# Linear-attention buffers moved out of the conv history's bytes, conv halves written later, and the sample rows' conv as products and one sum

## The reference

```python
za, zq, zk, zv, zg, zr = split_cols(z, [2 * D_CONV, GLA_DK, GLA_DK, GLA_DV, GLA_DV, GLA_RANK])
ya, conv_new = conv_module(za, conv_prev, conv_w, conv_b, conv_ln_g, conv_ln_b)
yb, gla_new = gla_mixer(zq, zk, zv, zg, zr, gla_prev, gla_w_gate, gla_b_gate, gla_g_norm)
return jnp.concatenate([ya, yb], axis=-1), conv_new, gla_new
```

## Time and profile before

| | |
|---|---|
| time, median of 3 runs | 2952.89 us (2947.61 to 2955.87) |
| time of the profiled execution | 2945.37 us |
| its span in the profile | 2943.7 us |
| PE busy | 2768.6 us (94%) |
| DVE busy | 1397.8 us (47%) |
| ACT busy | 1162.7 us (39%) |
| granted clock of PE, mean | 0.949 |

### The profile page before, as it was taken

The page is one execution under the profiler, slowest core; times in us unless marked ns, Lnnn a source line. Parts: engine busy times, 40 slices in busy tenths (PEclk is TensorE's granted clock), DMA queues, the critical chain, the costliest instruction groups (busy, mean ns, idle before and its releaser), DMA issues.

```text
span 2943.7 us, 48112 instructions
## 1 busy us (share of the span) xinstructions
PE 2768.6 (94%) x20153; PEld 2534.3 (86%) x20153; DVE 1397.8 (47%) x2026; ACT 1162.7 (39%) x1488; POOL 86.1 (3%) x116
## 2 busy tenths in 40 slices
PE   5899967989999999999999899889899999999998
PEld 1788955878888888898999899579899999999998
DVE  1699736344444433444444445534545544444444
ACT  2333254234343322334433445433544433444433
POOL 1000000010000000000000000001000000000000
PEclk7999986899999999999999999589999999999999
DMA  9677782675777688777644444114344434444343
GB/s 400 269 274 277 277 140 100 247 271 219 280 286 284 257 322 319 284 281 283 229 147 157 164 165 150 35 55 172 118 167 171 152 139 178 168 162 171 138 164 130
DMA packets 75771, 603.50 MB, mean 205 GB/s; under 512 B 21029, under 2 KB 22373, under 8 KB 24050
## 3 DMA queue, kind: packets, MB, share of 16 engines
q1 hardware_dynamic: 75634, 601.54, 55.8%
HBM read 592.01 MB, written 9.49 MB: 204 GB/s over the span
## 4 chain that ended last, share of the span: by engine, by line
PE 85%; DVE 5%; DMA 4%; ACT 3%; issue 2%; SPq 1%; POOL 1%; DVEq 0%; POOLq 0%; ACTq 0%
PE ps L599 25%; PE ps L601 24%; PE ps L600 24%; PE ps L625 5%; DMA pre_ring<-in_w_ada 2%; DMA aring<-in_w_ada 2%; DVE w_lo L1321 1%; DVE cacc L1410 1%; PE ps L610 1%; PE ps L841 1%; SPq L456 1%; ACT tn L1135 1%; ACT w_hi L979 1%; PE ps L638 0%; POOL ssq L553 0%
## 5 line engine op out<-in xcount | busy, mean ns | idle before, releaser
L1321 DVE TENSOR_TENSOR w_lo<-raw,w_hi 128x2048 fp32r<-128x2048 f32 (+1 forms) x402 | 835.6, 2080 | 1156.3 <-ACT w_hi L979 1156.3
L599 PE MATMUL ps<-act_hi,w_hi 128*128 128x288 f32 x4352 | 1303.3, 299 | 46.0 <-DVE act_lo L1508 30.9
L600 PE MATMUL ps<-act_hi,w_lo 128*128 128x288 f32 x4352 | 1288.7, 296 | 0.0
L601 PE MATMUL ps<-act_lo,w_hi 128*128 128x288 f32 x4352 | 1283.9, 295 | 0.0
L979 ACT ACTIVATE w_hi<-raw 128x2048 fp32r<-128x2048 f32 (+1 forms) x402 | 699.5, 1741 | 1110.2 <-PE ps L601 1104.2
L599 PEld LDWEIGHTS ps<-act_hi,w_hi 128*128 128x128 f32 x4352 | 820.2, 188 | 107.0 <-issue 91.7
L601 PEld LDWEIGHTS ps<-act_lo,w_hi 128*128 128x128 f32 x4352 | 823.9, 189 | 0.0
L600 PEld LDWEIGHTS ps<-act_hi,w_lo 128*128 128x128 f32 x4352 | 821.9, 189 | 0.0
L599 PE MATMUL ps<-hid_hi,w_hi 128*128 128x288 f32 x1408 | 420.5, 299 | 8.6 <-DVE w_lo L1321 8.6
L600 PE MATMUL ps<-hid_hi,w_lo 128*128 128x288 f32 x1408 | 416.7, 296 | 0.0
L601 PE MATMUL ps<-hid_lo,w_hi 128*128 128x288 f32 x1408 | 415.3, 295 | 0.0
(11 more groups left out here) (264 smaller groups left out, 1401.4 us busy)
## 6 DMA issues: line engine op xcount, KB each, us to landing
aring<-in_w_ada SPq DMA_DIRECT2D x176, 1024.0 KB, 7.9
raw<-in_w_gu SPq DMA_DIRECT2D x88, 2048.0 KB, 8.2
raw<-in_w_dn SPq DMA_DIRECT2D x64, 1408.0 KB, 5.9
raw<-in_w_ab SPq DMA_DIRECT2D x20, 2048.0 KB, 8.0
raw<-in_w_out SPq DMA_DIRECT2D x16, 2048.0 KB, 8.3
raw<-in_w_cd SPq DMA_DIRECT2D x13, 2048.0 KB, 8.2
pre_ring<-in_w_ada SPq DMA_DIRECT2D x16, 1024.0 KB, 9.4
aring<-in_state_glaT SPq DMA_DIRECT2D x4, 1024.0 KB, 9.2
```

The source lines that it names most:

```text
L599: pe.matmul(bank, w_hi[:, h, cols], hi[:, kt, :], start=begin, stop=False)
L600: pe.matmul(bank, w_lo[:, h, cols], hi[:, kt, :], start=False, stop=False)
L601: mm = pe.matmul(bank, w_hi[:, h, cols], lo[:, kt, :], start=False, stop=end)
L1321: dve.tensor_tensor(w_lo[:, h, 0:w], raw[:, par, h * w:(h + 1) * w], w_hi[:, h, 0:w].bitcast(F32), ALU.subtract).then_inc(split_done, 1)
```

## The change

Four things are changed.

1. The GLA buffers lie in `w_hi[:, 1]` and `w_lo[:, 1]`, the second places of the split weights, which hold nothing between the last z step and the output projection. The waits for the conv's copies and stores ahead of the heads go. The split of the output projection's first second half moves from head 0 to behind head 3, behind waits for all stores.
2. The conv's result goes to `act_hi` and `act_lo` in head 0, behind the gate of head 1 (`conv_high`, `conv_low`), where that split was. SP issues the conv stores behind the state loads of heads 0 and 1.
3. In the conv, a tile's sample columns are made by 4 products of 8 x 31 (one for each new token) into `taps_prod`, one sum over the taps and one addition of the bias, in place of 31 instructions. The prompt columns keep 31, each of which now adds to the result of the one just ahead of it.
4. Squares, `stat`, `rstd` and the affine of the layer norm move ahead by about a step; squares have four slots; the affine of the sample columns goes to DVE (`samples_affine`); loops over 8 sequences become one instruction.

```diff
--- before.py
+++ after.py
...
             free_lo = sb("free_lo", [P, KT * T], stack=a)
...
         raw = sb("raw", [P, 2, SLOT])
-        w_hi = sb("w_hi", [P, 2, SLOT // 2], F32R)
-        w_lo = sb("w_lo", [P, 2, SLOT // 2], F32R)
+        with ExitStack() as a:
+            w_hi = sb("w_hi", [P, 2, SLOT // 2], F32R, stack=a)
+        with ExitStack() as a:
+            sb("under_w_hi1", [P, SLOT // 2], stack=a)
+            gs = sb("gs", [P, 4, 256], stack=a)
+            vtok = sb("vtok", [P, 2, 256], stack=a)
+            os_tok = sb("os_tok", [P, 2, 256], stack=a)
+        sb("w_hi_home", [P, SLOT])
+        with ExitStack() as a:
+            w_lo = sb("w_lo", [P, 2, SLOT // 2], F32R, stack=a)
+        with ExitStack() as a:
+            sb("under_w_lo1", [P, SLOT // 2], stack=a)
+            vtok_s = sb("vtok_s", [P, 256], stack=a)
+            kltok = sb("kltok", [P, 2, P], stack=a)
+            klm = sb("klm", [P, 2, P], stack=a)
+            att = sb("att", [P, 2, P], stack=a)
+            att_s = sb("att_s", [32, 32], stack=a)
+            rowmask = sb("rowmask", [P, 2], stack=a)
+        sb("w_lo_home", [P, SLOT])
         aring = sb("aring", [P, 2, 4 * ADA_N])
...
-        with ExitStack() as a:
-            sb("under_z", [P, 24 * T], stack=a)
-            gs = sb("gs", [P, 4, 256], stack=a)
-            vtok = sb("vtok", [P, 2, 256], stack=a)
-            os_tok = sb("os_tok", [P, 2, 256], stack=a)
...
+        def square_of(q):
+
+            if isinstance(q, int) and SQUARES[1] <= q < SQUARES[2]:
+                return (sqb[:, 0], sqb[:, 1], sg[:, 0], sg[:, 1])[q % 4]
+            return sqb[:, q % 2]
...
-                sp.wait_ge(conv_ready, CT)
-                sp.dma_start(o["conv_p"], uext[:, :, NP_TOK:UW]).then_inc(conv_stored, 16)
-                for j in range(CT):
-                    sp.dma_start(o["conv_s"][:, j], rows_s(j)[:, :, TS:SW]).then_inc(conv_stored, 16)
                 for h in range(HEADS):
...
+                    if h == 1:
+                        store_conv()
                     if h >= 1:
                         store_states(h - 1)
                 store_states(HEADS - 1)
                 sp.wait_ge(state_stored, 16 * HEADS)
+
+            def store_conv():
+
+                sp.wait_ge(conv_ready, CT)
+                sp.dma_start(o["conv_p"], uext[:, :, NP_TOK:UW]).then_inc(conv_stored, 16)
+                for j in range(CT):
+                    sp.dma_start(o["conv_s"][:, j], rows_s(j)[:, :, TS:SW]).then_inc(conv_stored, 16)
...
-                    if seg.kind == "z" and ls == 2:
-                        stat()
...
+                    if seg.kind == "z" and ls == 1:
+                        stat()
...
-            def conv_squares():
-                for j in range(CT):
+            def conv_squares(js):
+                for j in js:
                     q = 16 + j
-                    wait_square(q)
-                    act.activation(sqb[:, q % 2, 0:NP_TOK], y_all[:, j], ACT.Square)
-                    act.activation(seqs(sqb[:, q % 2, NP_TOK:T]), y_all_s[:, j], ACT.Square).then_inc(sq_ready, 1)
+                    act.wait_ge(sq_added, q - 3)
+                    act.activation(square_of(q)[:, 0:NP_TOK], y_all[:, j], ACT.Square)
+                    act.activation(seqs(square_of(q)[:, NP_TOK:T]), y_all_s[:, j], ACT.Square).then_inc(sq_ready, 1)
...
-                    for y in (y_all[:, j], y_all_s[:, j]):
-                        ins = act.activation(y, y, ACT.Identity, scale=vec[:, gj:gj + 1], bias=vec[:, bj:bj + 1])
+                    y = y_all[:, j]
+                    ins = act.activation(y, y, ACT.Identity, scale=vec[:, gj:gj + 1], bias=vec[:, bj:bj + 1])
                 ins.then_inc(conv_affined, 1)
...
+                    if seg.kind == "z" and ls == 1:
+                        act.wait_ge(centred, 1)
+                        conv_squares(range(4))
+                    if seg.kind == "z" and ls == 2:
+                        act.wait_ge(normed, 1)
+                        conv_affine()
                     if nxt:
                         split(nxt, n + 1, 1 - par, 0)
+                    if seg.kind == "z" and ls == 1:
+                        conv_squares(range(4, CT))
...
-                        stat_rstd(CT * P)
-                        act.wait_ge(normed, 1)
-                        conv_affine()
+                        act.wait_ge(conv_affined, 2)
+                        for k in range(2):
+                            conv_silu(k)
...
-                        act.wait_ge(centred, 1)
-                        conv_squares()
...
+                        stat_rstd(CT * P)
...
                 gate_terms(0)
-
-                act.wait_ge(conv_y, CT // 2)
-                act.activation(act_hi[:, 0:CT, 0:NP_TOK], y_all, ACT.Copy)
-                for s in range(NSEQ):
-                    ins = act.activation(act_hi[:, 0:CT, NP_TOK + TS * s:NP_TOK + TS * (s + 1)], y_all_s[:, :, s], ACT.Copy)
-                ins.then_inc(mixhi_done, CT)
                 gate_exps(0)
 
-                act.wait_ge(act_ready, KT + CT)
-                act.wait_ge(conv_stored, 16 * (CT + 1))
...
-                        split(after, after.n0, after.n0 % 2, 1)
+                        conv_high()
...
+                act.wait_ge(gstate_stored, 16 * HEADS)
+                act.wait_ge(conv_stored, 16 * (CT + 1))
+                split(after, after.n0, after.n0 % 2, 1)
...
+                acc = cacc[:, 0:NP_TOK]
+                acc_s = cacc[:, NP_TOK:T].rearrange("p (t b) -> p t b", b=NSEQ)
                 if 0 in taps:
                     if not (isinstance(j, int) and j == 0):
                         dve.wait_ge(conv_ready, j)
                     if L.n:
                         L.wait(L.n)
+                    ws = vec[:, bass.ds(j * TAPS + w, TAPS)].unsqueeze(1).to_broadcast([P, NSEQ, TAPS])
+                    for at_t in range(TS):
+                        ins = dve.tensor_tensor(taps_prod[:, at_t], rows_s(j)[:, :, at_t:at_t + TAPS], ws, ALU.mult)
+                    marks[1] = L.mark(ins)
                 for k in taps:
                     wk = flat_at(vec, j * TAPS + (w + k))
-                    for s in range(2):
-                        row = taps_s(j, k) if s else at(uext, j, k, k + NP_TOK)
-                        acc = seqs(cacc[:, NP_TOK:T]) if s else cacc[:, 0:NP_TOK]
-                        out = acc if k < TAPS - 1 else taps_s(j, 0) if s else at(uext, j, 0, NP_TOK)
-                        if marks[s]:
-                            L.wait(marks[s])
-                        if k == 0:
-                            ins = dve.tensor_scalar(out, row, wk, flat_at(vec, j + VEC["conv_b"]), ALU.mult, ALU.add)
-                        else:
-                            ins = dve.scalar_tensor_tensor(out, row, wk, acc, ALU.mult, ALU.add)
-                        if k == TAPS - 1 and s:
-                            ins.then_inc(conv_ready, 1)
-                        else:
-                            marks[s] = L.mark(ins)
+                    row = at(uext, j, k, k + NP_TOK)
+                    if k == 6:
+                        L.wait(marks[1])
+                        marks[1] = L.mark(dve.tensor_reduce(acc_s, taps_prod[:], AX.X, ALU.add))
+                    if k == 16:
+                        L.wait(marks[1])
+                        dve.tensor_scalar(taps_s(j, 0).rearrange("p b t -> p t b"), acc_s, flat_at(vec, j + VEC["conv_b"]),
+                                          None, ALU.add)
+                    if k == 0:
+                        marks[0] = L.mark(dve.tensor_scalar(acc, row, wk, flat_at(vec, j + VEC["conv_b"]), ALU.mult, ALU.add))
+                        continue
+                    L.wait(marks[0])
+                    if k < TAPS - 1:
+                        marks[0] = L.mark(dve.scalar_tensor_tensor(acc, row, wk, acc, ALU.mult, ALU.add))
+                    else:
+                        dve.scalar_tensor_tensor(at(uext, j, 0, NP_TOK), row, wk, acc, ALU.mult, ALU.add).then_inc(conv_ready, 1)
...
-                    if seg.kind == "z" and ls == 2:
-                        for k in range(2):
...
+                    if seg.kind == "z" and ls == 1:
+                        dve.wait_ge(rstd_ready, 2)
+                        apply_stat(y_all, y_all_s, rstd, ALU.mult).then_inc(normed, 1)
+                        samples_affine()
...
-                for s in range(NSEQ):
-                    cols = by[:, NP_TOK + TS * s:NP_TOK + TS * (s + 1)].unsqueeze(1).to_broadcast([P, CT, TS])
...
+                return dve.tensor_tensor(y_s, y_s, seqs(by[:, NP_TOK:T]).unsqueeze(1).to_broadcast([P, CT, NSEQ, TS]), op)
...
+                gj, bj = VEC["conv_ln_g"], VEC["conv_ln_b"]
+                rows = y_all_s
+                dve.wait_ge(normed, 1)
+                g, b = (vec[:, k:k + CT].unsqueeze(2).unsqueeze(3).to_broadcast([P, CT, NSEQ, TS]) for k in (gj, bj))
+                L.link(dve.tensor_tensor(rows, rows, g, ALU.mult))
```

(13 more changed lines are left out.)

39 lines of the change are left out of this document (15 added, 24 removed).

## The result

The changed kernel takes 2924.14 us, the median of 4 runs (2921.99 to 2930.57), against 2951.52 for the kernel before on the same chip (2947.61 to 2955.87). The ratio is 0.991, 95% interval 0.9888 to 0.9932: faster by 0.9%. The profiled execution took 2922.46 us where that of before took 2945.37, 22.9 less; the forecast for it was 2920.7, and for the median 2928.2, 4 above what was measured.

What follows compares the result with a forecast made beforehand. PE was taken as the bound, busy nearly throughout, so other engines' edits pay only where PE waits. Terms -9.1 - 18.2 + 0.7 + 0 + 0.5 + 1.4 = -24.7 turn the median 2952.9 into 2928.2 us; range 2920 to 2940.

Steps and rivals of the forecast that it cites:

- Layer norm earlier: First mixer's z steps: PE no longer waits 5.2 us for POOL's sum, `adarow` and the drain come earlier; -9.1 us.
- signs listed: Trace observations named beforehand as showing the prediction right or wrong, such as PE waiting over 8 us for `w_lo`.
- The wait for the stores: Ahead of head 0: `vtok` follows the gate's exponentials directly instead of waiting for the conv stores; -18.2 us.
- SP's order: State loads go ahead of the conv stores; head 1's `gs` write meets the stores' end; +0.5 us, bounds 0 to +10.
- The rival of 2938: Stores come back as a wait inside the heads: head 1's `gs` waits 10 us; 2938 us, chance 0.12.
- Head 0: Conv copies replace a split of the same 2048 columns, plus one 256-column instruction each on ACT and DVE; +0.7 us.
- The split at the end: Split moved behind head 3 is ready before PE needs it, with 6 us of cover; nothing added.
- The conv on DVE: First 16 taps take 10.3 to 10.4 us against 9.0, delaying PE in the opening; +1.4 us.
- DVE becomes the bound in the gate steps: Rival: sums and products at the scan's rate cost 2.7 us more a tile; +9.8 us, 2938 us, chance 0.07.
- links are free: Rival: chained conv taps on DVE cost nothing extra, only instruction count matters; -26.4 us, 2926.5 us, chance 0.08.
- last rival: The wait ahead of the heads was not for the stores, so they start as late; 2944 us, chance 0.01.

Runs made afterwards that it cites:

- buffers only: Kernel before with the new GLA buffers, new SP order, conv parts behind head 1's gate and moved split, old layer norm and conv: 2933.52 us, ratio 0.9949.
- old conv: Changed kernel with the taps of prefix and samples in turns, as in the kernel before: 2922.78 us, ratio 0.9913.
- stores first: Changed kernel, its buffers kept, with SP's nine conv stores ahead of the two state loads again: 2945.51 us, ratio 0.9991.
- late products: Changed kernel with the samples' products between taps 24 and 27 and their sum ahead of tap 28: 2923.02 us, ratio 0.9899.
- parts ahead: Conv's high and low parts ahead of head 0 again: changed kernel 2923.54 us, ratio 0.9914; with late products and prefix taps in two sums, 2917.87 us, 0.9896.
- old norm's place: Changed kernel with two square buffers, `stat` a step later, sample affine on ACT and normalization in step 2: 2934.2 us, ratio 0.9959.
- second profile: Changed kernel, nothing altered, run and profiled once more on another chip: 2928.0 us, ratio 0.9913 of the kernel before.

## Why the prediction was right

**Layer norm earlier, -9.1.** Right. A to B shows 9.19 between the changed kernel and the one with the old place, and 9.05 between buffers only (295.97) and old conv (286.92), which differ in this alone there. The affine took 4.04 where I had put 4, and `adarow` began at 404.35, where the sum's 401.4, the 2.2 of the conv and a start 0.7 later give 404.3. Of the signs listed, `adarow` was to come 7 to 8 us earlier than before and came 6.1 earlier, and head 0's keys near 418 came at 419.63: both misses are the conv's term and that start.

**The wait for the stores, -18.2.** Right: B to C fell by 18.36. That it was the stores' the view of ACT didn't say (its 18.18 us stand as "issue"); DVE's waits in the kernel before, from 443 us on, do, for its own first write into those bytes:

```profile
DVE att L1605 <- DMA out_conv_s<-uext: 14.8, 1, 14.8
```

What I had not weighed is how much of it SP's new order carries. I priced that order as a small cost, +0.5, and gave no rival in which it was left as it was; the kernel with the stores first shows 19.00 us on it.

**SP's order, +0.5 with 0 to +10 as bounds.** It cost nothing. The stores' end was put at 444 and the last thing in that queue, `gs`, landed at 444.4; but head 1 wrote `gs` at 448.09 and not at 444.9, as head 0 began and ran later than in the sum. So the two did not meet, by 3.7 us. The rival of 2938, with chance 0.12, had the stores end 10 us later; by these rows that would have cost 6 and not 10. It was nearer than the result tells: in the other eight traces with this order `gs` is written 0.8 us (late products) to 9.3 us (buffers only) after its store has landed, always behind a wait for PE.

**Head 0, +0.7.** Right for the work, though the head grew by 1.35 (21.43 to 22.78). The rest is the granted clock, which the sum had no term for. The eight products of values and keys at the start of the head show it, in the kernel before and in the changed one:

```profile
447.74 1.13 PE L776 MATMUL ps<-vtok,kltok 64*128 64x256 f32 x8
```

```profile
423.38 1.71 PE L800 MATMUL ps<-vtok,kltok 64*128 64x256 f32 x8
```

In the rows of stretches the granted clock was 1.00 there in the kernel before, and 0.65 in the changed one:

```profile
447.70:448.90 1.20, 1.20 (x13) 0.79 (x9) 0.00 (x0) 1.01 (x2) 0.00 (x0) 1.00 0.00 0
```

```profile
423.40:425.10 1.70, 1.70 (x10) 1.20 (x9) 0.00 (x0) 1.53 (x3) 0.00 (x0) 0.65 1.78 34
```

These eight are in the chain: DVE's copy to `gs` waits for them. They take 1.14 to 2.08 us in the seven traces with the same head, and C to D less their time is 20.98 to 21.07 in all seven, which explains the spread of the table. In the kernel before it is 21.43 - 1.13 = 20.30, so the conv parts cost 0.77. With the parts ahead it is 20.13 and 20.49; the 0.36 between these two lies in PE's outputs behind the eight, from its first product of `att` to its first of `klm`: 6.82 us (431.24 to 438.06) and 7.18 (423.65 to 430.83), the first 0.8 us at a granted clock of 1.00 and of 0.81.

**The split at the end, nothing.** Right: the low half was done at 510.60, PE wanted it behind the pair of 514.55.

**The conv on DVE, +1.4.** This is the term that was mis-sized: it is +2.2 (289.12 - 286.92), and +2.3 by the other pair (298.31 - 295.97). Each instruction was priced rightly. What failed is the step "so the front-loaded 1.4 delays PE there": it counted the first tile's 16 taps and stopped. With it went a slip in the sum, "in all of a tile it is 17.6 against 17.3": 10.4 for the first 16 taps, 15 x 0.51 for the rest and the bias make about 18.1. DVE's timeline has 10.42 + 2.11 + 5.60 = 18.13 for the first tile, against 17.30 before, so a tile costs 0.8 more and not 0.3. PE's stops in the opening before were 2.69 and 1.50, beside a common one of 1.39; now they are 4.20, 1.16 and 1.07, as PE's timeline of the changed kernel has them:

```profile
134.99 0.58 PE L623 MATMUL ps<-act_hi,w_hi 128*128 128x288 f32 x1 [4.20 <-DVE w_lo L1348]
...
156.86 0.40 PE L623 MATMUL ps<-act_hi,w_hi 128*128 128x288 f32 x1 [1.16 <-DVE w_lo L1348]
...
164.59 0.37 PE L623 MATMUL ps<-act_hi,w_hi 128*128 128x288 f32 x1 [1.07 <-DVE w_lo L1348]
```

The first grew by 1.5. The second tile has its products in front as well, ahead of a low half that PE also waits for, and that was left out. DVE's timeline shows it; first the changed kernel, then the same `w_lo` before:

```profile
148.27 1.39 DVE L1430 TENSOR_TENSOR taps_prod<-uext,vec 128x248 f32<-128x248 f32 x4
...
162.16 2.29 DVE L1348 TENSOR_TENSOR w_lo<-raw,w_hi 128x2048 fp32r<-128x2048 f32 x1
```

```profile
159.22 2.28 DVE L1321 TENSOR_TENSOR w_lo<-raw,w_hi 128x2048 fp32r<-128x2048 f32 x1
```

From the start of the first tile's conv to there are 162.16 - 122.14 = 40.02 us against 159.22 - 121.42 = 37.80, so 2.2 more. Piece by piece: +1.50 for the first 16 taps, -0.67 for the rest of the first tile, +1.80 for the second tile's first piece with its products and sum, -0.43 for its next taps. Over the first two tiles DVE is the bound, so the whole sum of its work between two low halves counts, not only what is front-loaded; the late products tell the same in another way. PE's stops are no measure of the delay by themselves: with the same conv, old norm's place and stores first have three stops that sum to 6.7 us, without the one of 1.16, since PE ran at a granted clock of 0.78 and 0.75 from 138 to 146 us.

That the loss ended there was luck. DVE's period of two gate steps, 28.9 us before, is now 186.32 - 156.72 = 29.6, against PE's 29.7:

```profile
156.72 0.45 DVE L1383 SCALAR_TENSOR_TENSOR sg<-ps,sg 128x288 f32<-128x288 f32 x1
...
186.32 0.45 DVE L1383 SCALAR_TENSOR_TENSOR sg<-ps,sg 128x288 f32<-128x288 f32 x1
```

The prediction wrote that 0.3 more fits; 0.7 did, with 0.1 to spare. The rival in which DVE becomes the bound in the gate steps, at chance 0.07, needed no price like the scan's, only a little more than what was measured.

The rival in which the links are free is refuted by the 0.513 against 0.395 of the two chains. The Trainium skill, "VectorE: DVE Perf Modes", section "The DRAIN you can't avoid", has a semaphore between chained operations cost nothing extra; the measurement, 0.12 us a link, decides against it.

**The sum.** -9.1 + 2.2 - 18.4 + 1.4 = -23.9 up to head 0's store, as A to D shows. The heads 1 to 3 took 0.3 less, the start 0.7 more, all behind the last head 0.4 more: -23.0, the difference of the spans, against -24.7 forecast. The misses are 0.8 in the conv's term, 0.65 in head 0, nearly all of it clock, and 0.85 outside A to D, less 0.5 for SP's order, which did not come, and 0.15 more from the stores' wait. A slip without weight: the last rival's 2944 should be 2928.2 + 18.2 = 2946.4. The medians on that chip differ by 27.4, on the chip of the second profile by 24.0; that these lie on either side of 24.7 says no more than that runs of one kernel lie 8 us apart and more.

## What to carry to other kernels

Where an engine waits for a transfer, look for the second transfer behind it in the same queue before pricing the first: here the new buffers without the new order turned 18 us of waiting for stores into 19 us of waiting for a load. When a chain of accumulations is long, use two accumulators in turns: the link costs 0.12 us per instruction of 256 elements only where neighbours depend on each other, so that fewer instructions in one chain can be slower than more in two. And where an engine is the bound over several steps, cost all its work between the deadlines of the other engine, not only what is moved to the front.

## What the runs showed of the hardware

- Stores of 120 KB in packets under 512 B hold up their queue: eight took 22.18 to 30.66 us to issue in these kernels and landed, at the median, 13.9 us after their issue in the changed kernel. Loads of 1 MB issued right behind them took 14.0 to 14.8 us to land (stores first), the two issued right ahead of them 9.6 and 13.7, and the one for head 2, issued when they had landed, 4.8 (both in the changed kernel). The store of `gs` behind them took 3.35 us to issue, where that of the next head took 0.33.
- The same eight matmuls took 1.13 to 2.08 us in the same place, by the moment at which the granted clock came back from 0.50, to which it had fallen after PE stood still ahead of the heads (3.2 us in the changed kernel, 21.6 before).
- A reduction over 992 elements to 32 takes 1.18 us, as a reduction of 64 in 0.22 and 1.04 ns for each element more, both from the rows of before, had given (1.19).
- The same program began its first low half at 115.23 and at 120.78 in two profiles, and from the store of the last head's states to the end it took 2417.5 and 2424.4 us, 7.0 apart. I have no cause for either; whole-run times of this kernel can't show terms of 2 us.
